# Splitting the input projection of a hybrid decoder layer into products of high and low parts

## What is computed

```
sh_m, sc_m, g_m, sh_f, sc_f, g_f = split(silu(c) @ w_ada + b_ada, 6)        # w_ada 1024 x 6144
h = rms_norm(x, norm_mix) * (1 + sc_m) + sh_m                               # 512 + 8 rows x 1024
z = h @ w_in                                                                # w_in 1024 x 1280
q, k, v, u = split(z, [512, 640, 768])
q, k = rms_norm(q per head of 64), rms_norm(k per head of 64)
attention over the last 128 positions, score + rel_bias[bucket(distance)]; pooling mixer over u
```

## Time and profile before

| | us |
|---|---|
| median of 3 runs | 1344.97 (1343.53 to 1345.5) |
| the profiled execution | 1345.92 |
| its span, first to last instruction | 1344.3 |
| TensorE busy | 1209.0 (90%) |
| VectorE busy | 679.4 (51%) |
| ScalarE busy | 489.0 (36%) |
| GpSimd busy | 327.3 (24%) |
| mean granted TensorE clock | 0.946 of 2.4 GHz |

### The profile page before, as it was taken

How to read it: one execution, slowest core, us unless ns; L and a number is a source line. 1 busy time by engine, 2 the same in 40 slices (tenths; PEclk the granted TensorE clock), 3 DMA queues, 4 the chain that set the end, 5 groups by cost and what they waited for, 6 DMA issues and landing times.

```text
span 1344.3 us, 17518 instructions
## 1 busy us (share of the span) xinstructions
PE 1209.0 (90%) x6382; PEld 719.3 (54%) x6382; DVE 679.4 (51%) x1067; ACT 489.0 (36%) x703; POOL 327.3 (24%) x354
## 2 busy tenths in 40 slices
PE   5799799969999979999899979998979998999974
PEld 2354465543675735755575347555447556465631
DVE  1331433472785874553694235536535527576631
ACT  5112342221564633332573133324323324455430
POOL 2205330031222313112322411133412124131311
PEclk8999799979999989999899999998979998999996
DMA  9966545398999999999999999999999899999994
GB/s 333 377 141 207 216 150 211 127 362 351 407 396 354 409 406 394 403 384 361 403 413 406 403 394 403 392 362 406 408 389 406 350 352 409 411 408 414 403 407 183
DMA packets 92735, 474.25 MB, mean 353 GB/s; under 512 B 17824, under 2 KB 20287, under 8 KB 43440
## 3 DMA queue, kind: packets, MB, share of 16 engines
q1 hardware_dynamic: 73120, 444.61, 82.5%
q0 software_dynamic: 18752, 26.63, 8.4%
q10 hardware_dynamic: 776, 1.87, 0.4%
HBM read 459.57 MB, written 32.66 MB: 366 GB/s over the span
## 4 chain that ended last, share of the span: by engine, by line
PE 54%; DMA 14%; DVE 6%; issue 2%; ACT 1%; POOL 1%; SPq 1%; POOLq 0%; DVEq 0%; ACTq 0%
PE bank L2398 51%; DMA raw<-in_w 7%; DVE rawr L2218 2%; DMA out_y_prompt<-gu,slot_tok 2%; DMA yd<-gu,idx_s 2%; PE bank L2446 1%; DMA yd<-ost,idx_s 1%; PE bank L2422 1%; POOL gu L1909 1%; ACT hi L2035 1%; DVE gu L2182 1%; SPq L544 1%; DVE gu L2180 0%; DVE ost L2252 0%; ACT ost L2018 0%
## 5 line engine op out<-in xcount | busy, mean ns | idle before, releaser
L2218 DVE TENSOR_TENSOR rawr<-raw,hi 128x1024 fp32r<-128x1024 f32 x288 | 351.7, 1264 | 107.0 <-ACT hi L2035 105.3
L2035 ACT CAST hi<-raw 128x1024 fp32r<-128x1024 f32 x288 | 294.7, 1048 | 167.1 <-PE bank L2398 140.5
L1895 POOL DMA_INDIRECT yd<-ost,idx_s x31 | 56.4, 1818 | 326.5 <-ACT ost L2018 325.6
L2398 PE MATMUL bank<-raw,xT_even 128*64 128x512 f32 (+1 forms) x704 | 135.2, 600 | 0.1
L2398 PE MATMUL bank<-raw,aT 128*32 128x256 f32 (+1 forms) x992 | 114.3, 481 | 12.7 <-DMA raw<-in_w 12.6
L2398 PE MATMUL bank<-raw,xT_odd 128*32 128x512 f32 (+1 forms) x544 | 84.9, 644 | 14.4 <-DMA raw<-in_w 14.4
L2398 PE MATMUL bank<-hi,xTh_odd 128*128 128x512 f32 x224 | 76.6, 424 | 22.4 <-DVE rawr L2218 22.3
L2398 PE MATMUL bank<-hi,xTh_even 128*128 128x512 f32 x256 | 84.5, 412 | 5.1 <-DVE rawr L2218 5.1
L2398 PE MATMUL bank<-hi,aTh 128*128 128x512 f32 x240 | 77.4, 404 | 12.2 <-DVE rawr L2218 12.2
L2180 DVE TENSOR_SCALAR gu<-bank 128x512 f32<-128x512 f32 (+1 forms) x50 | 31.4, 628 | 102.9 <-PE bank L2398 102.9
L2000 ACT ACTIVATE gu<-gu 128x512 f32<-128x512 f32 (+1 forms) x50 | 29.2, 583 | 146.5 <-DVE gu L2180 146.5
(11 more groups left out here) (386 smaller groups left out, 1797.1 us busy)
## 6 DMA issues: line engine op xcount, KB each, us to landing
raw<-in_w SPq DMA_DIRECT2D x356, 1024.0 KB
raw<-in_w SPq DMA_DIRECT2D x48, 512.0 KB
raw<-in_w_ada SPq DMA_DIRECT2D x21, 1024.0 KB, 13.3
w_in_sb<-in_w_in SPq DMA_DIRECT2D x4, 1280.0 KB, 27.7
w_out_sb<-in_w_out SPq DMA_DIRECT2D x4, 1024.0 KB, 9.1
early<-in_w SPq DMA_DIRECT2D x4, 1024.0 KB, 11.9
ada_more<-in_w_ada SPq DMA_DIRECT2D x3, 1024.0 KB, 22.9
xs<-in_x_prompt SPq DMA_DIRECT2D x4, 512.0 KB, 15.0
```

What stands on the lines that cost most here:

```text
L1895: gp.indirect_dma_start(yd_of[n], bass.IndirectOffsetOnAxis(ap=m.idx_s[:, p % 6, b:b + 1], axis=0), out_rows(p, b), None, bounds_check=lim ...
L2035: nc.scalar.copy(m.hi[:, (2 * n + h) % HI, :], m.raw[:, slot, h * D:(h + 1) * D]).then_inc(hi_done, 1)
L2218: v.tensor_tensor(m.rawr[slot][:, half], m.raw[:, slot, half], m.hi[:, (2 * n + h) % HI, :].bitcast(F32), ALU.subtract).then_inc(lo_done, 1)
L2398: return nc.tensor.matmul(out, lhsT, rhs, start=start, stop=stop, skip_group_check=True)
```

## The change

Half modulation: the first eight units are cut so that units 0 to 3 hold the shift and scale of features 0 to 511, and 4 to 7 those of the rest; each unit is two transfers with rows of 2 KB. After units 0 to 3 one half is turned and k = 0 to 3 are projected, first for row blocks 0 and 1, then, between units 4 to 7, for 2 and 3. Then the second half follows in the same way.

Split products: h and w_in are each split into a high part (a cast on ScalarE) and a low part (a subtraction on VectorE, written over the f32 original), and each product becomes three. Six banks take the sums of all four row blocks at once: 4 to 7 for q, 2 and 3 for k and v of two blocks each. The samples stay f32 (`project_samples`), in bank 0.

x is normalised on VectorE instead of ScalarE. The line of biases is stored once and read back by one DMA whose access pattern makes overlapping slices; that turns the tokens of a block around, so q and the attention output are turned with a flipped identity, by a f32 product instead of a transpose. b1 and b2 land as 128 x 768, in eight loads, and 32 stores bring them to DRAM. The q and k norms run in the order of row blocks 0, 1, samples, 2, 3.

```diff
+ADA, WHOLE = 24, 8
 ADA_RAW = (0, 1, 2, 5)
-ADA_SLOTS, ADA_MORE = len(ADA_RAW), 3
+ADA_MORE = (68928, 81216, 89600, 41216)
+ADA_PLACE = [0, 1, 4, 2, 3, 5, 6, 7] + [2, 3] * 3 + [0, 1, 2, 3] * 2 + [0, 1]
+CHAIN = [0, 1, TP, 2, 3]
...
+        m.hTh = at("hT_high", [P, KC, SEQ], F32R, raw0)
+        m.w_in_low = at("w_in_low", [P, KC, IN_W], F32R, wproj0)
+        m.w_high = (at("w_high_a", [P, 4, 768], F32R, H0 + 68928), at("w_high_b", [P, 4, 768], F32R, H0 + 89600))
+        m.u_high = [at(f"u_high{g}", [P, KC, P], F32R, place)
+                    for g, place in enumerate((raw0 + 6 * SLOT_B, raw0 + 6 * SLOT_B + 4096, H0 + 68928, H0 + 73024))]
...
+    ada_bank = (bank[3], bank[1])
+    u_bank = (bank[1], bank[5], bank[2], bank[5])
+    def kv_cols(t):
+        return bank[2 + t // 2][:, 256 * (t % 2):256 * (t % 2) + 256]
+    def q_rows(t):
+        return bank[4 + t][:] if t < TP else m.zs_q[:]
+    def k_rows(t):
+        return m.k_raw[:, t, :] if t < TP else m.zs_k[:, 0:KVW]
...
+                if n < WHOLE:
+                    half, u = n // 4, n % 4
+                    for kk in range(2):
+                        k = 2 * u + kk
+                        src = i["w_ada"][0, k * P:(k + 1) * P, 0:2 * D].rearrange("p (s h n) -> h p s n", s=2, h=2)
+                        sp.dma_start(ada_unit(n)[:, kk * D:(kk + 1) * D].rearrange("p (s n) -> p s n", s=2), src[half]
...
+            load_x(0)
+            load_ada(0)
+            load_x(1)
+            load_x(2)
+            load_ada(1)
+            load_x(3)
+            load_x(TP)
+            load_ada(2)
+            load_ada(3)
+            load_w_in(0)
+            load_w_in(1)
+            for n in range(4, WHOLE):
+                load_ada(n)
+            load_w_in(2)
+            load_w_in(3)
             for n in range(WHOLE, ADA):
+                if n == 14:
+                    sp.wait_ge(s.u_ready, 4)
                 load_ada(n)
-                if n == 17:
-                    sp.wait_ge(s.z_ready, TT)
-                    sp.wait_ge(s.u_ready, 4)
+                if n == 18:
...
+            gp.wait_ge(s.bb_lo_done, 1)
+            for l, part in enumerate((m.bb_hi, m.bb_lo)):
+                for k in range(4):
+                    rows = slice(NE * k, NE * k + NE)
+                    up, down = part[rows, 0:512], part[rows, 512:768]
+                    gp.dma_start(m.bd[:, 2 * k + l, :], up).then_inc(s.bb_out, 16)
+                    gp.dma_start(m.bd[:, 8 + 2 * (k // 2) + l, 256 * (k % 2):256 * (k % 2) + 256], down
+                                 ).then_inc(s.bb_out, 16)
+                    sec, q = k // 2, 2 * (k % 2)
+                    of = m.bd_32.rearrange("e (q l) c -> l e q c", l=2)[l]
+                    gp.dma_start(of[:, q:q + 2, 256 * sec:256 * sec + 256], up.rearrange("e (j c) -> e j c", j=2)
+                                 ).then_inc(s.bb_out, 16)
+                    gp.dma_start(of[:, 4 + k, :].rearrange("e (s c) -> e s c", s=2),
+                                 down.unsqueeze(1).to_broadcast([NE, 2, 256])).then_inc(s.bb_out, 16)
+            gp.wait_ge(s.line_out, 16)
+            gp.wait_ge(s.bb_out, BB_ALL)
+            gp.dma_start(m.bias[:], bass.AP(m.lines.tensor, m.lines.offset, [[1, P], [LINE, NH], [1, 2 * P]])
+                         ).then_inc(s.bias_in, 16)
+            gp.wait_ge(s.u_ready, 2)
             gp.dma_start(m.Kc[:], ck.rearrange("b j g d -> j b (g d)")).then_inc(s.kv_in, 16)
             gp.dma_start(m.Vc[:], cv.rearrange("b j g d -> j b (g d)")).then_inc(s.kv_in, 16)
-            gp.wait_ge(s.skew_out, 16)
...
+            def w_highs(k):
+                if not k % 4:
+                    act.wait_ge(s.ada_used, 4 if not k else WHOLE)
+                act.wait_ge(win_in[k // 2], 16)
+                nc.scalar.copy(m.w_high[k // 4][:, k % 4, :], m.w_in[:, k, 0:768]).then_inc(s.w_high_ready, 1)
+            def h_highs(k):
+                act.wait_ge(s.h_ready, k + 1)
+                nc.scalar.copy(m.hTh[:, k, :], m.hT[:, k, 0:SEQ]).then_inc(s.h_high_ready, 1)
+            def u_highs(g):
+                if not g:
+                    act.wait_ge(s.line_ready, 1)
+                if g == 2:
+                    act.wait_ge(s.zs_done, 5)
+                for n in range(4):
+                    act.wait_ge(win_in[n], 16)
+                nc.scalar.copy(m.u_high[g][:], m.w_in[:, :, 768 + g * P:768 + (g + 1) * P]).then_inc(s.u_high_ready, 1)
...
+            def modulated(k):
+                v.tensor_scalar(m.hT[:, k, 0:SEQ], m.hT[:, k, 0:SEQ], m.g1T[:, k, 8:9], m.modT[:, k, 8:9],
+                                ALU.mult, ALU.add).then_inc(s.h_ready, 1)
+            def w_lows(k):
+                v.wait_ge(s.w_high_ready, k + 1)
+                v.wait_ge(s.zs_done, k + 1)
+                v.tensor_tensor(m.w_in_low[:, k, 0:768], m.w_in[:, k, 0:768],
+                                m.w_high[k // 4][:, k % 4, :].bitcast(F32), ALU.subtract).then_inc(s.w_low_ready, 1)
+            def h_lows(k):
+                v.wait_ge(s.h_high_ready, k + 1)
+                v.tensor_tensor(m.hTl[:, k, 0:SEQ], m.hT[:, k, 0:SEQ], m.hTh[:, k, :].bitcast(F32),
+                                ALU.subtract).then_inc(s.h_low_ready, 1)
+            def u_lows(g):
+                v.wait_ge(s.u_high_ready, g + 1)
+                v.wait_ge(s.zs_done, KC)
+                cols = slice(768 + g * P, 768 + (g + 1) * P)
+                v.tensor_tensor(m.w_in_low[:, :, cols], m.w_in[:, :, cols], m.u_high[g][:].bitcast(F32),
+                                ALU.subtract).then_inc(s.u_low_ready, 1)
...
+            for h in range(2):
+                mod_half(h)
+                for k in range(4 * h, 4 * h + 4):
+                    modulated(k)
+                    if k % 4:
+                        w_lows(k - 1)
+                        h_lows(k - 1)
+                w_lows(4 * h + 3)
+                h_lows(4 * h + 3)
+            u_lows(0)
+            u_lows(1)
...
+            def turn_mod(h):
+                pe.wait_ge(s.mr_ready, h + 1)
+                pe.wait_ge(s.blank, 3)
+                for b in range(4):
+                    last = mm(ada_bank[h][:, 18 * b:18 * b + 18], m.mod_rows[:, h, b * P:(b + 1) * P],
+                              m.pair_sum[:].rearrange("p s n -> p (s n)"), start=True, stop=True)
+                last.then_inc(s.mt_tr, 1)
...
+                    if t < TP:
+                        mm(bank[0][:, c * P:(c + 1) * P], m.qn[:, c * P:(c + 1) * P], m.flip[:], start=True, stop=True)
+                    else:
+                        tr(bank[0][:, c * P:c * P + R], m.qn[0:R, c * P:(c + 1) * P], m.ident[0:R, 0:R])
...
+            def project_samples(k):
+                pe.wait_ge(win_in[k // 2], 16)
+                pe.wait_ge(s.h_ready, k // 4 * 4 + 1)
+                for g in range(4):
+                    last = mm(bank[0][32 * g:32 * g + NS, 0:320], m.hT[:, k, SEQ:TOK],
+                              m.w_in[:, k, 320 * g:320 * g + 320], start=(k == 0), stop=(k == KC - 1))
+                last.then_inc(s.zs_done, 1)
+            def project(k, pair):
+                pe.wait_ge(s.w_low_ready, k + 1)
+                pe.wait_ge(s.h_low_ready, k + 1)
+                w_hi, w_lo = m.w_high[k // 4][:, k % 4, :], m.w_in_low[:, k, 0:768]
+                for t in pair:
+                    h_hi, h_lo = m.hTh[:, k, tok(t)], m.hTl[:, k, tok(t)]
+                    for n, (x, w) in enumerate(((h_hi, w_hi), (h_hi, w_lo), (h_lo, w_hi))):
+                        first, final = not k and not n, k == KC - 1 and n == 2
+                        mm(bank[4 + t][:], x, w[:, 0:512], start=first, stop=final)
+                        last = nc.tensor.matmul(kv_cols(t), x, w[:, 512:768], start=first and not t % 2, stop=final,
+                                                skip_group_check=True)
+                if k == KC - 1:
+                    last.then_inc(s.z_ready, 1)
+            def project_u(g):
+                pe.wait_ge(s.u_low_ready, g + 1)
+                if g == 1:
+                    pe.wait_ge(s.qk_ready, 2)
+                    pe.wait_ge(s.vt_ready, 2)
+                if g == 3:
+                    pe.wait_ge(s.U_ready, 2)
+                for k in range(KC):
+                    hi, lo = m.u_high[g][:, k, :], m.w_in_low[:, k, 768 + g * P:768 + (g + 1) * P]
+                    mm(u_bank[g][:], hi, m.hTh[:, k, :], start=(k == 0), stop=False)
+                    mm(u_bank[g][:], hi, m.hTl[:, k, 0:SEQ], start=False, stop=False)
+                    last = mm(u_bank[g][:], lo, m.hTh[:, k, :], start=False, stop=(k == KC - 1))
+                last.then_inc(s.u_ready, 1)
+            ada(0)
+            turn_x(0)
+            turn_x(1)
+            ada(1)
+            turn_x(2)
+            bias_lines()
+            ada(2)
+            turn_x(3)
+            turn_x(TP)
+            ada(3)
+            turn_mod(0)
+            for k in range(4):
+                project_samples(k)
```

(84 more changed lines are left out.)

437 lines of the change are left out of this document (197 added, 240 removed).

## The result

The changed kernel takes 1361.7 us (median of 4 runs, 1359.55 to 1362.88) where the kernel before takes 1344.65 us: ratio 1.0125, 95% interval 1.0109 to 1.0141. It is 17 us slower; 1338 us was forecast, with 1348 us as the upper end of the range. A second set on another chip gave 1360.55 us, ratio 1.0120 (1.0096 to 1.0144). The ratios given are not quite the quotients of the medians beside them.

A forecast was written before the change was run, and what follows sets the result against it. Input projection bound by TensorE, expert stage by DMA; start 29.3 us plus 93.9 us puts the transposes at 123.2 us, 8.2 us earlier; less 1.3 us in attention, net 6.9 us: forecast 1338 us, range 1328 to 1348 us.

The forecast's parts named there:

- the transposes: Sample-state transposes, TensorE's last work before the scores: forecast at 123.2 us, 8.2 us ahead of 131.37 us.
- start of the first samples' product: Start of the projection, set by the landing of w_in's first piece: forecast at 29.3 us.
- chained half 1: First four of the eight chained k steps, row blocks 0 and 1: forecast 18.9 us.
- chained steps: Row blocks 0 and 1, where products wait for VectorE's in-place subtraction: 4.7 us per k, TensorE idle about 1.8 us.
- first rival: Clock falls to 1.2 GHz in the chained steps: 1349 us for four cold steps, 1360 us for eight; chance 0.13.
- The modulation loads: Modulation units 4 to 13 within the projection: 10 x 1.0 us of TensorE, 10.0 us, no load wait counted.
- The rival of a late start: Projection doesn't begin earlier, pieces or x late: 2 to 4 us less gain, 1341 us; chance 0.08.
- The attention stage: After the sample-state transposes: the same except turning attention by four f32 products, 1.3 us counted.
- The eight waits: TensorE's gaps ahead of project(k), released by VectorE's h_low: eight of 1.5 to 2 us.
- that rival: A 256-column product costs as much as a 512-column one, 0.228 us: 11 us more, 1349 us; chance 0.05.
- GpSimd's queue: Small bias stores, slices, cache loads, pooling sums: hidden by 4 us; as rival becoming last, 1342 to 1345 us, chance 0.07.
- The prediction's own sign of being wrong: Granted clock reading 0.50 in the chained steps, where 1.00 was forecast from 32 to 120 us.

The follow-up runs named there:

- gaps_filled: Changed kernel with six unused f32 products of 128 columns behind each samples' product, where TensorE waited: 1350.12 us, ratio 1.0060 to the kernel before.
- gaps_half_filled: Changed kernel with three unused f32 products of 128 columns behind each samples' product: 1351.23 us, ratio 1.0060 to the kernel before.
- after_again: The changed kernel, unedited, run again with a second profiled execution: 1360.55 us, ratio 1.0120 to the kernel before.
- all_f32: Changed kernel's order, banks and early start, but every projection product in f32, without split products: 1344.27 us, ratio 1.0008 to the kernel before.
- unit10_slot: Changed kernel with modulation units 10 and 13 loaded into a third place, not those of units 8 and 9: 1353.55 us, ratio 1.0084.
- start_filled: Changed kernel with samples' products a step ahead, units 10 and 13 in a third place, samples' pooling sums later, eleven filling products at the start: 1329.72 us, ratio 0.9892.
- samples_ahead: Changed kernel with each samples' product issued one step ahead of the row blocks' products, within each half: 1339.44 us, ratio 0.9963 to the kernel before.

## Why the prediction was wrong

Five stretches add up to the miss at the transposes, forecast against the profiled execution:

| stretch | forecast, us | measured, us | miss |
|---|---|---|---|
| start of the first samples' product | 29.3 | 31.66 | +2.4 |
| chained half 1 (31.66 to 56.23) | 18.9 | 24.6 | +5.7 |
| units 4 to 7, half of row blocks 2 and 3, turning | 12.7 | 13.4 | +0.7 |
| chained half 2 (69.62 to 93.44) | 18.9 | 23.8 | +4.9 |
| from there to the transposes at 141.94 | 43.4 | 48.5 | +5.1 |

**The step that failed: the clock in the chained steps.** The steps were priced at 4.7 us, at full clock; at full clock they take 4.84 us. The row blocks' products of six of the eight steps ran partly or wholly at 1.2 GHz. Filling the pauses gave back 8.0 us in the two halves; with the first steps, which stayed slow in gaps_filled, the clock makes some 9.9 us of the 10.6 us that the halves missed (an estimate: 48.4 us less twice the 19.25 us of gaps_filled's second half, which ran at full clock). The prediction had this as its first rival, with a sum (1349 us for four cold steps, 1360 us for eight) and gave it 0.13. That the kernel ended at the upper of these times is chance: the rival put 21.6 us on the clock in the steps, and the clock took less than half of it; the loads, the start and the stretch behind the transposes made up the rest. The row that it was dismissed by, full clock at 30 to 32 us with TensorE busy 0.97 of 2.00 us, was one stretch of transposes and units with short pauses; in the steps, one pause of 1.85 us and a burst alternate. gaps_half_filled has such rows too, busy 1.02 of 2.00 us at 38 to 40 us at full clock, in steps that do hold. One row at full clock is no evidence on a pattern with longer pauses, and not even on its own: in the second execution of the kernel before the same stretch is at full clock too, and the clock then falls (columns as in the earlier trace rows):

```profile
30.00:32.00 2.00, 0.83 (x16) 1.00 1.00 415
...
38.00:40.00 2.00, 1.51 (x4) 0.50 1.01 410
```

The Trainium skill's page "TensorE: Matmul & The Clock Gate", section "A second HAM failure mode: psum-queue depth-cycling", tells of such micro-idles between groups of matmuls, in a bf16 kernel and without saying how long they were; after_again's rows (pauses of 1.85 us, clock 1.00, then 0.80 and 0.50) agree with it, and it should have had the larger chance.

**The chain itself was never worth its price, by the forecast's own numbers.** A chained step was put at 4.7 us. The same step in f32 is 2.58 us of row blocks and 0.56 us of samples, 3.1 us (3.43 us measured in all_f32). So the chain was forecast to cost 8 x 1.6 = 12.8 us, more than the 4.2 us and 6.2 us that the same prediction has the split save in row blocks 2 and 3 and in the pooling columns. The 1.8 us of idle in each step were written down and then not compared with doing it otherwise. In the prediction's sum the whole gain comes from starting 10.0 us earlier. all_f32 shows what that gives: 3.9 us of head and nothing that can be measured at the end.

**The modulation loads.** Units were priced by TensorE's 1.0 us. Units 10 and 11 are loaded where 8 and 9 lie, so their load is asked for only behind the use of these: 4.1 us of waiting, and products at 1.2 GHz behind the second wait. unit10_slot took 5.7 us back in that stretch, which is the whole of the last row of the table.

**The start.** The products began 2.4 us late. w_in's first piece had landed by 29.02 us, where ScalarE's cast that waited for it starts (29.3 us was forecast), but it did not set the start. The last of the four units started at 26.41 us, behind TensorE's turns of the last blocks of x, and not at 24.5 us as forecast; from there to the end of the first modulated block it took 5.1 us, not 4.2 us, with TensorE waiting 0.81 and 1.56 us for VectorE and turning the modulation at 1.2 GHz (1.81 us, 0.96 us in the second half). The rival of a late start (0.08) had the size right and another cause. These pauses cost the clock as well (start_filled: 4.3 us earlier at the transposes, where 2 to 3 us were expected).

**Behind the transposes.** The attention stage was taken as the same. It wasn't: sums that VectorE did beside another part of GpSimd's pooling before now met its additions, 3.88 us of waiting where 1.00 us was, and the clock fell once more in it and once in the products with w_out (32.4 us to the first transposes of h where the kernel before took 30.75 us).

**What was right.** The eight waits of 1.5 to 2 us released by hT_low (1.83 to 1.86 us); split products at full clock, 0.23 us for 512 columns and 0.12 us for 256 (0.11 us forecast), so that rival is dead; turning a row block, 1.03 us (1.26 us); a pooling group, 5.55 us (5.5 us); GpSimd's queue, whose 32 small stores lasted from 93.00 to 109.4 us and whose bias slices were issued at 111.38 us, with no wait of VectorE on them: hidden, as forecast, though the stores began 12 us and the slices 4 us later than forecast. The head's loss does reach the end, +12.6 us at the first product with w_out and 17 us at the median; for a gain that holds only in part (samples_ahead: 12 to 14 us at the transposes, 3.3 and 6.9 us at the median). The prediction's own sign of being wrong, the clock at 0.50 in the steps, is what the trace shows.

## What to carry to other kernels

Price a dependency that a change adds against the whole work of the same step done the old way, not only against the products that it speeds up, and issue the short product that frees a buffer one step ahead. Where a kernel bound by TensorE gets a pause of nearly 2 us in every step, reckon the products behind it at half the clock, in part at least, until a trace shows otherwise: here pauses of 0.98 us cost nothing beyond themselves, and eight of 1.85 us (14.8 us) cost 8 us more. Filling products in such pauses are a cheap test of that, and at the start of the projection they were worth keeping. And a load into the place of a unit that is used late is a wait, however short TensorE's own work on it is.

## What the runs showed of the hardware

- In the chained steps the granted clock reads 1.00 through a pause of 1.85 us and falls in the burst behind it, in most steps but not in all (after_again: two of eight 4.83 and 4.84 us long); six small f32 products per pause, or three, keep it at 1.00.
- VectorE's two-operand additions stand still to the end of GpSimd's two-operand operation (1.15 us beside it), not beside its one-operand one (0.19 us).
- Executions of one kernel differ by up to 15 us at the end (samples_ahead: 1329.92 to 1344.83 us over ten) with projections that repeat within 2 us.
